# The gate projection placed inside the decode attention of a hybrid decoder step

## The reference

```python
h = rmsnorm(x, norm_pre_mix)
q_f, k_f, v_f, f_logit, q_d, k_d, v_d = split(h @ w_in)          # 8 fox heads, 3 x 4 dilated heads, 128 wide
o_fox = softmax(q_f k_f^T / sqrt(128) + forget bias) @ v_f        # sample: 2048 cached tokens in 16 pages of 128, per request
o_dil = windows (128,1), (512,4), (2048,16), merged by their denominators
g_fox, g_dil = split(sigmoid(h @ w_gate + b_gate))                # 2048 x 4096
m = (g_fox * (o_fox @ w_o_fox) + g_dil * (o_dil @ w_o_dil)) @ w_out
x = x + rmsnorm(m);  y = x + rmsnorm(swiglu(rmsnorm(x)))          # 2048 x 11264, 5632 x 2048
```

## Time and profile before

| what | value |
|---|---|
| median of 3 runs | 2866.8 us (2862.89 to 2868.53) |
| the profiled execution, its own time | 2874.63 us |
| its span, first to last instruction | 2872.7 us |
| mean granted clock | 0.919 |
| PE busy | 88 % of the span |
| DVE, ACT, POOL busy | 36 %, 30 %, 14 % |
| moved by DMA | 574.66 MB |

### The profile page before, as it was taken

The page is one execution under the profiler, slowest core; times in us unless marked ns, Lnnn a source line. Parts: engine busy times, 40 slices in busy tenths (PEclk is TensorE's granted clock), DMA queues, the critical chain, the costliest instruction groups (busy, mean ns, idle before and its releaser), DMA issues.

```text
span 2872.7 us, 46489 instructions
## 1 busy us (share of the span) xinstructions
PE 2515.9 (88%) x18285; PEld 2246.4 (78%) x18285; DVE 1048.4 (36%) x1391; ACT 857.5 (30%) x970; POOL 408.2 (14%) x846
## 2 busy tenths in 40 slices
PE   5799579995599968888888789689999999899996
PEld 4799369994499954454554789489999999899995
DVE  1343224432233433333332453533333333344444
ACT  2123112331034422322222222334343343333322
POOL 1000000001100024443343000001111111022210
PEclk8699569997599989999999899899999999999998
DMA  6144104552044359999999454347767666578881
GB/s 169 58 153 154 53 30 146 161 155 94 21 124 146 117 180 361 366 379 340 349 349 384 134 175 155 107 154 240 240 233 243 235 234 228 196 240 278 288 274 58
DMA packets 332581, 574.66 MB, mean 200 GB/s; under 512 B 19251, under 2 KB 277579, under 8 KB 328479
## 3 DMA queue, kind: packets, MB, share of 16 engines
q1 hardware_dynamic: 263520, 269.62, 29.8%
q0 software_dynamic: 68960, 303.67, 29.5%
HBM read 558.77 MB, written 104.10 MB: 231 GB/s over the span
## 4 chain that ended last, share of the span: by engine, by line
PE 75%; DMA 9%; issue 5%; DVE 5%; ACT 2%; POOL 2%; POOLq 2%; SPq 0%; DVEq 0%; ACTq 0%
PE ps L638 20%; PE ps L639 20%; PE ps L640 20%; DMA kraw<-in_cache_fox_k 4%; PE ps L647 2%; PE ps L809 2%; DMA kraw<-in_cache_win_k 1%; DMA vraw<-in_cache_fox_v 1%; POOLq L534 1%; PE ps L814 1%; PE ps L899 1%; PE ps L834 1%; ACT w_hi L1005 1%; DMA d_h<-scratch_hankel 1%; DMA raw<-in_w_down 1%
## 5 line engine op out<-in xcount | busy, mean ns | idle before, releaser
L638 PE MATMUL ps<-act_hi,w_hi 128*128 128x320 f32 x3136 | 976.8, 311 | 31.1 <-DVE act_lo L1307 22.5
L1278 DVE TENSOR_TENSOR w_lo<-raw,w_hi 128x2048 fp32r<-128x2048 f32 (+2 forms) x276 | 582.7, 2112 | 1088.4 <-ACT w_hi L1005 1088.4
L639 PE MATMUL ps<-act_lo,w_hi 128*128 128x320 f32 x3136 | 973.2, 310 | 0.0
L640 PE MATMUL ps<-act_hi,w_lo 128*128 128x320 f32 x3136 | 972.8, 310 | 0.0
L1005 ACT ACTIVATE w_hi<-raw 128x2048 fp32r<-128x2048 f32 (+2 forms) x276 | 487.9, 1769 | 993.5 <-PE ps L640 975.3
L638 PEld LDWEIGHTS ps<-act_hi,w_hi 128*128 128x128 f32 x3136 | 592.7, 189 | 32.1 <-issue 32.1
L639 PEld LDWEIGHTS ps<-act_lo,w_hi 128*128 128x128 f32 x3136 | 592.6, 189 | 0.0
L640 PEld LDWEIGHTS ps<-act_hi,w_lo 128*128 128x128 f32 x3136 | 592.4, 189 | 0.0
L1508 DVE COPY kT<-ps 128x512 f32<-128x512 f32 x176 | 121.8, 692 | 280.2 <-PE ps L814 280.2
L1150 ACT ACTIVATE kT<-ps 128x512 f32<-128x512 f32 x184 | 109.8, 597 | 323.6 <-PE ps L809 323.5
L809 PEld LDWEIGHTS ps<-ident,kraw 128*128 128x128 f32 x736 | 80.3, 145 | 154.8 <-DMA kraw<-in_cache_fox_k 78.8
(11 more groups left out here) (305 smaller groups left out, 2597.6 us busy)
## 6 DMA issues: line engine op xcount, KB each, us to landing
raw<-in_w_gate_up SPq DMA_DIRECT2D x88, 1024.0 KB, 7.4
kraw<-in_cache_fox_k POOLq DMA_DIRECT2D x128, 512.0 KB, 7.7
vraw<-in_cache_fox_v POOLq DMA_DIRECT2D x128, 512.0 KB, 7.9
raw<-in_w_in SPq DMA_DIRECT2D x60, 1024.0 KB, 7.6
raw<-in_w_gate SPq DMA_DIRECT2D x32, 1024.0 KB, 6.6
raw<-in_w_down SPq DMA_DIRECT2D x32, 1024.0 KB, 5.9
out_win_k_sample<-in_cache_win_k POOLq DMA_DIRECT2D x64, 510.0 KB, 5.8
out_win_v_sample<-in_cache_win_v POOLq DMA_DIRECT2D x64, 510.0 KB, 3.9
```

The source lines that it names most:

```text
L638: pe.matmul(ps[:, bk_, 0:T], w_hi[:, slot, k, :], xh[:, x_k, :], start=(k == k0), stop=False)
L639: pe.matmul(ps[:, bk_, 0:T], w_hi[:, slot, k, :], xl[:, x_k, :], start=False, stop=False)
L640: mm = pe.matmul(ps[:, bk_, 0:T], w_lo[:, slot, k, :], xh[:, x_k, :], start=False, stop=(k == k1 - 1))
L1278: dve.tensor_tensor(w_lo[:, slot, 0:kt, :], raw[:, pslot, 0:kt, P * half:P * half + P], w_hi[:, slot, 0:kt, :].bitcast(F32), ALU.subtract) ...
```

## The change

The gate units leave their stage and are placed whole after steps of decode: two in sequence 0 and in sequence 8, four in each other one, so at steps 5, 11, 17, 23 (11, 23 for two). A unit's result goes through a two-slot tile gst to DRAM; the sigmoid reads PSUM with the bias in the same instruction. A unit's weight split is in two halves, after the next step and after the one behind it. Panels all use raw's slot 0. act_hi, act_lo, raw slot 0, w_hi and w_lo stay whole, so decode's tiles move elsewhere: the key ring has 3 slots, the value ring 4 (in raw's slot 1). The attention output is kept as one fp32 tile, o32; its prompt part is split to o_hi and o_lo in sequence 8, the rest at the end. The o units' gates are loaded from DRAM by POOL into four slots. In the diff `gate_part` is PE's, last in each step of `sequence`; `gate_out` and `gate_split` are ACT's, and DVE has the same `gates_after` with its subtraction in place of the cast. `prompt_lo` is called at steps 5 to 7 of sequence 8, after ACT's `prompt_hi`.

```diff
-        o_hi = sb("o_hi", [P, HF + HG, T], F32R, M0 + 20480)
-        o_lo = sb("o_lo", [P, HF + HG, T], F32R, M0 + 35840)
+        o32 = sb("o32", [P, HF + HG, T], F32, M0 + 20480)
+        o_hi = sb("o_hi", [P, HF + HG, T], F32R, X0)
+        o_lo = sb("o_lo", [P, HF + HG, T], F32R, X0 + 16384)
...
-        KRING, VRING = 4, 8
+        KRING, VRING = 3, 4
+        vraw = sb("vraw", [P, VRING, 1024], F32, B0 + 57344)
+        gst = sb("gst", [P, 2, T], F32, Y0 + 9216)
+        gl = sb("gl", [P, 4, 2, T], F32, M0 + 35840)
-        gates = sb("gates", [P, 2 * KT, T], F32, X0)
...
+        GATE_UNITS = (2, 4, 4, 4, 4, 4, 4, 4, 2)
+        def gate_work(q, n):
+            u0, units = U_GATE + sum(GATE_UNITS[:q]), GATE_UNITS[q]
+            ended = range(units * n // STEPS, units * (n + 1) // STEPS)
+            return [(u0 + m, k) for m in ended for k in range(KT)]
+        def gates_done(q, n, late):
+            return [U_GATE + m for m, step_ in enumerate(GATE_DONE) if step_ + 1 + late == STEPS * q + n]
...
-            stream(U_GATE, 2 * KT, lambda i, s: (w_gate, i * 512 + 256 * s))
-            sp.wait_ge(o_ev, DB)
+            for p in range(KT):
+                for u in range(U_GATE + 2 * p - 4, U_GATE + 2 * p - 2):
+                    if u >= U_GATE:
+                        sp.wait_ge(acc_free, u + 3)
+                        sp.dma_start(gsc[u - U_GATE], gst[:, u % 2, :]).then_inc(g_st[u % 2], 16)
+                load_panel(0, U_GATE + 2 * p, [(0, cols_of(w_gate, 256 * p, 0, 8)), (8, cols_of(w_gate, 256 * p, 8, KT))])
...
+            sp.wait_ge(pv_done, DB * KPG)
+            load_panel(1, U_O, [(0, wof[:, :, 256:512]), (8, wod[:, :, 256:512])])
...
-            pool.wait_ge(acc_free, U_O + 2)
-            pool.wait_ge(zero_ok, 1)
+            pool.wait_ge(lo_done, U_GATE)
...
             def load_bias(b):
+                pool.wait_ge(zero_ok, 1)
...
+            pool.wait_ge(g_st[0], 16 * KT)
+            pool.wait_ge(g_st[1], 16 * KT)
...
+            with pool.Fori(0, KT // 4) as i:
+                for k in range(4):
+                    pool.wait_ge(acc_free, i * 4 + (U_O + k - 1))
+                    pool.dma_start(gl[:, k], halves[bass.ds(i * 4 + k, 1)].rearrange("e p o t -> p (e o) t")).then_inc(g_ld[k], 16)
...
+            def gate_part(q, n):
+                for u, k in gate_work(q, n):
+                    if k == 0:
+                        pe.wait_ge(lo_done, u + 1)
+                        pe.wait_ge(acc_free, u + 1)
+                    acc = ps[:, u % 2, 0:T]
+                    pe.matmul(acc, w_hi[:, u % 2, k, :], act_hi[:, k, :], start=(k == 0), stop=False)
+                    pe.matmul(acc, w_hi[:, u % 2, k, :], act_lo[:, k, :], start=False, stop=False)
+                    mm = pe.matmul(acc, w_lo[:, u % 2, k, :], act_hi[:, k, :], start=False, stop=(k == KT - 1))
...
-            pe.wait_ge(o_ev, DB)
+            pe.wait_ge(acc_free, U_O + 2)
+            pe.wait_ge(o_sp, 1)
...
+            def gate_out(u):
+                act.wait_ge(unit_done, u + 1)
+                wait_pos(act, g_st[u % 2], 16 * ((u - U_GATE) // 2))
+                act.activation(gst[:, u % 2, :], ps[:, u % 2, 0:T], ACT.Sigmoid,
+                               bias=cols[:, 64 + u - U_GATE:65 + u - U_GATE]).then_inc(acc_free, 1)
+            def gate_split(u, late):
+                if not late:
+                    act.wait_ge(raw_ld[0], loads(U_GATE) + 32 * ((u - U_GATE) // 2 + 1))
+                ks = slice(8, KT if u < U_O else KO) if late else slice(0, 8)
+                act.activation(w_hi[:, u % 2, ks, :], raw[:, 0, ks, P * (u % 2):P * (u % 2) + P], ACT.Copy).then_inc(hi_done if late else g_half, 1)
+            def gates_after(q, n):
+                for u in gates_done(q, n, 0):
+                    gate_out(u)
+                    gate_split(u + 2, False)
+                for u in gates_done(q, n, 1):
+                    gate_split(u + 2, True)
...
-            def out_parts(h, src, done):
-                link(dve.tensor_copy(hi, src))
-                dve.tensor_tensor(lo, src, hi.bitcast(F32), ALU.subtract).then_inc(done, 1)
+            def keep_out(h, src, done):
+                dve.tensor_copy(o32[:, bass.ds(h, 1), 0:SEQ].rearrange("p o n -> p (o n)"), src).then_inc(done, 1)
...
+            def prompt_lo(c):
+                dve.wait_ge(os_h, c + 1)
+                part = (slice(None), slice(4 * c, 4 * c + 4), slice(0, SEQ))
+                dve.tensor_tensor(o_lo[part], o32[part], o_hi[part].bitcast(F32), ALU.subtract)
...
+                    dve.wait_ge(g_ld[k], i * 16 + 16)
+                    dve.tensor_tensor(a1, ps[:, k, 0:T], gl[:, k, 0, :], ALU.mult)
```

More of the change, by code:

```diff
@@ L795, in _ @@
             pe.wait_ge(pre_ok, 1)
[L798 to L801 removed]
+            def gate_part(q, n):
[7 more added lines that the diff above has]
+                    mm = pe.matmul(acc, w_lo[:, u % 2, k, :], act_hi[:, k, :], start=False, stop=(k == KT - 1))
+                    if k == KT - 1:
+                        mm.then_inc(unit_done, 1)
             def transposes(b, s):
@@ L929, in turn_out, with sequence @@
                 mm.then_inc(o_tr, 1)
-            def sequence(kb, vb):
-                for n in range(KPG + 1):
+            def sequence(q, kb, vb):
+                for n in range(STEPS):
                     if kb is not None and n < KPG:
@@ L1127, in _ @@
                     act.activation(d_pt[:], ps[:, 3 + g, 0:384], ACT.Copy).then_inc(pd_pc, 1)
-            def gate_trip(i, last):
-                for k in range(4):
-                    if last and k >= 2:
-                        act.wait_ge(unit_done, i * 4 + (U_GATE + k + 1))
-                    else:
-                        step(i * 4 + (U_GATE + k), k, i * 32 + loads(U_GATE))
-                    act.wait_ge(acc_free, i * 4 + (U_GATE + k + 3))
-                    g = gates[:, bass.ds(i * 4 + k, 1), :].rearrange("p o n -> p (o n)")
-                    act.activation(g, g, ACT.Sigmoid).then_inc(g_sig, 1)
-            with act.Fori(0, 2 * KT // 4 - 1) as i:
-                gate_trip(i, False)
-            gate_trip(2 * KT // 4 - 1, True)
+            def gate_out(u):
[14 more added lines that the diff above has]
+                    gate_split(u + 2, True)
+            act.wait_ge(fb_st, 16 * DB)
             def keys_a(b, s):
@@ L1463, in _, with gate_split, gates_after @@
             dve.wait_ge(fb_st, 16 * DB)
-            def gate_trip(i, last):
-                for k in range(4):
-                    if last and k >= 2:
-                        dve.wait_ge(unit_done, i * 4 + (U_GATE + k + 1))
-                    else:
-                        step(i * 4 + (U_GATE + k), k)
-                    dve.tensor_scalar(gates[:, bass.ds(i * 4 + k, 1), :].rearrange("p o n -> p (o n)"), ps[:, k, 0:T],
-                                      cols[:, bass.ds(i * 4 + (k + 64), 1)], None, ALU.add).then_inc(acc_free, 1)
-            with dve.Fori(0, 2 * KT // 4 - 1) as i:
-                gate_trip(i, False)
-            gate_trip(2 * KT // 4 - 1, True)
+            def gate_split(u, late):
+                dve.wait_ge(hi_done, u + 1) if late else dve.wait_ge(g_half, u - U_GATE - 1)
+                ks = slice(8, KT if u < U_O else KO) if late else slice(0, 8)
+                ins = dve.tensor_tensor(w_lo[:, u % 2, ks, :], raw[:, 0, ks, P * (u % 2):P * (u % 2) + P],
+                                        w_hi[:, u % 2, ks, :].bitcast(F32), ALU.subtract)
+                if late:
+                    ins.then_inc(lo_done, 1)
+            def gates_after(q, n):
+                for u in gates_done(q, n, 0):
+                    gate_split(u + 2, False)
+                for u in gates_done(q, n, 1):
+                    gate_split(u + 2, True)
             dve.memset(pg[:], 0.0)
```

127 lines of the change are left out of this document (71 added, 56 removed).

## The result

The changed kernel takes 2893.9 us (median of 6 runs, 2883.1 to 2901.2), the kernel before 2867.3 in the same comparison: ratio 1.0087, 95% interval 1.007 to 1.0103. It is slower by 0.9 %, and the prediction (2820, range 2778 to 2872) has the wrong sign and misses the time by 74 us. The profiled execution took 2893.58 us.

A forecast was written before the change was run, and what follows sets the result against it. After the change TensorE (84 us a sequence) was to bound decode, with DMA (79) close behind. Savings 226.0 - 15 - 167 - 15 + 8.6 + 2.8 + 6.5 = 46.9 us, less 7.8 for the median, gave 2820 us, range 2778 to 2872.

The forecast's parts named there:

- Part 3: Decode sequences 1 to 7: walked six steps at a time to 88.6 us, plus 2.4, so 91 against 67.1; 167 us given back.
- Rival D: Decode: units not overlapping with transfers at all; ruled out because no ring slot waits for a unit; no chance given.
- The floors: Decode, per sequence: least time from each engine's own work, TensorE 84.1 us with four units, DMA about 79 us.
- Rival B: Decode: gate panel lands too late, ScalarE waits ahead of key evictions; 70 us more, 2890; chance 0.13.
- Rival C: Decode: shallow rings, each unit costs 3 us of a fresh landing; 96 us a sequence, 35 more, 2855; chance 0.12.
- Rival A: Decode: TensorE alone bounds, panel stalls vanish; 86 us a sequence, 35 us less, 2785; chance 0.22.
- Part 1: Before decode: the gate stage goes, first transpose near 800.3 instead of 1026.33, 226.0 us earlier.
- part 6: Prompt heads: out_parts becomes one copy, 12 x 0.54 = 6.5 us saved; the prompt's later split costs nothing, 6 at most.
- Part 2: Decode sequence 0, keys alone: two units add 14 us, smaller ring 5, refilling during a unit takes off 4; 15 more.
- Part 4: Decode sequence 8, values alone: two units 14.0 us, value ring of four 3, refill takes off 2; 15 more.
- Part 5: Turn from decode to o projection: 14.6 us becomes about 6, 8.6 saved, and 2.8 saved from low-clock matmuls.
- Table loads: Decode ScalarE: four loads of 1.28 us a sequence, about half exposed; with a drain 39 us more, 2859, chance 0.04.

The follow-up runs named there:

- e11: Changed kernel with gate units spread evenly over steps, splits after even units three steps later, and an eighth of each gate panel from the third on: 2788.0 us.
- e12: Changed kernel with units spread evenly, splits after even units three steps later, and key and value rings of 4 and 8 (act_hi used twice): 2772.8 us.
- e10: Changed kernel with an eighth of each gate panel from the third on and key and value rings of 4 and 8 (act_hi used twice): 2815.5 us.
- e1: Changed kernel loading only an eighth of each gate panel from the third on, all waits kept: 2866.5 us.
- e2: Changed kernel with one matmul of 48 in each gate unit, panels, splits and rings kept: 2828.5 us.
- e3: Changed kernel with key and value rings of 4 and 8 instead of 3 and 4 (act_hi used twice): 2927.4 us.
- e9: Changed kernel with an eighth of each gate panel from the third on and one matmul of 48 in each unit: 2711.8 us.
- e8: Kernel before with key and value rings of 3 and 4 instead of 4 and 8, nothing else: 2927.2 us.
- e7: Changed kernel with units' blocks spread evenly over the steps and splits after even units three steps later, whole panels, rings 3 and 4: 2805.0 us.
- e4: Changed kernel with Exp in place of Sigmoid on the gates, which leaves no table loads in decode: 2884.3 us.
- e6: Changed kernel with the weight split after each even unit three steps later, units still whole: 2878.0 us.
- e13: Kernel before with the value ring alone cut from eight slots to four, key ring kept at four: 2887.7 us.

## Why the prediction was wrong

**Part 3 is the step that failed**, with 53.9 of the 65.7 us by which the first projection matmul is late (1620.5 for 1554.8). It forecast that the seven sequences would give back 167 us of the gain, at 91 us each; they take 98.7. By the experiments, from the floor up: 85.2 floor (e11, e12), + 4.4 for whole units with rings of four and eight (e10), + 5.3 for rings of three and four (e1), + 3.8 for the panel (after). The first step holds two edits, the whole units and their early splits; the others hold one each. The order matters, as e2, e3 and e9 show, so these are prices along one path and not shares. In TensorE's own account the 13.5 us above the floor are 9.8 of idle time (98.7 - 88.9) and 3.7 of busy time more than the floor, for which I had nothing. The low clock can account for them: a mean granted clock of 0.95 over the sequences, between levels of 0.5 and 1 (1.2 and 2.4 GHz), is nearly 10 us of each at the lower level.

Within part 3: I had written that rings of three and four hold one unit's worth of DMA work, and charged 2.4 us for everything beyond the walk. The walk took each engine's sum over six steps, which is right only if the loads keep coming while TensorE is in a unit. They don't, since a slot is freed by TensorE and POOL issues in order (5.96 us without an issue at 994.72). Rival D said the opposite in so many words, that no ring slot waits for a unit; this was the mistake behind the walk. The ring's price in the kernel before is 7.2 us (e8) where I had 0. In sequence 0 I had priced the same cut at 1.8 us a step against 1.3; in the steady sequences I didn't ask.

**The floors held.** TensorE 85.2 against 84.1. For the DMA engines I had 79; 0.96 x 87.9 in e7 are 84, within a few us of TensorE's. So both were near their limit. That the two can run there together is shown by e12; what the prediction had no term for is what it takes.

**Rival B** had the right verdict and the right picture: the wait of ScalarE on raw<-in_w_gate, the eviction behind it, the panel started after the late split. Its turn-taking estimate of 26 us is for the 128 packets of a whole panel on each engine, and a whole panel takes 21.7 us here and 24.6 in e12, where the DMA engines are full. ScalarE comes for it after 20.7 us where I had 17 to 20, so it waits in 5 panels, at most 4.1 us, and not up to 9 in each. Its price was too high, 3.8 us a sequence here where I had 70 / 7 = 10; that its total of 2890 comes near the result is luck, and the rings' doing. In the flight of a panel some 1700 key and value packets of 4 KB pass beside some 2200 on the panel's queue in e12, and some 1280 beside 2100 in the changed kernel. The Trainium skill, DMA: Bandwidth & Descriptors, section Queues, rings and completion order, has each engine take turns between the queue rows packet by packet. The trace agrees that both share the engines; in its own packets the turns are not one for one, but not far from it in e12. **Rival C** was nearest in the number, 96 us a sequence, for a reason that is half right: the rings, but by the slots that a unit keeps occupied and not by a landing of 3 us after each. **Rival A**, 86 us, is what e11 and e12 reach, and e7 within 2 us, once both stalls are gone.

**Part 1 and part 6** held: 233.7 us against 232.5. **Part 2**: 5.2 us short; rings cost there what I said (e8 takes 58.6 where the kernel before takes 54.5), and by that sum the unit gave nothing back for refilling, the 4 us that I took off. This is one execution; e4 and e6 do the same sequence in 3.5 us less. **Part 4**: 7.6 short; the value ring costs 10.9 us at the end (e13) and not 3. **Part 5**: the turn held to 0.2 us, in part by luck. The last unit's sigmoid and the split behind it stand ahead of the last copies of o in the queues of ScalarE and VectorE and take 3.3 us of it (0.53, 0.95 and 1.83), for which I had nothing, and what I had listed takes less than I thought. The low clock did not go. **Part 7**: nothing seen. **Table loads**: e4 gives 1.4 us a sequence, within the 2.4.

Beside the kernel before, in the two profiled executions: 233.7 us earlier at the first transpose, then 20.5 later in sequence 0 (76.2 for 55.7), 220.9 in the seven (690.9 for 470), 22.6 in sequence 8 (54.6 for 32), and 8.8 and 2.2 earlier at the turn and after it. That is 19.3 us slower, and the spans are 2892.0 and 2872.7. Taken by the marks alone the seven sequences are 216 us longer (98.7 for 67.8); the other 4.7 come from the boundaries 1082 and 1552, which are not at the marks of the kernel before.

What stays open: the 4.4 us of whole units with deep rings (e10) are 3.5 of idle time, most of it behind late key evictions by the two rows above, and 0.9 of busy time at a mean clock of 0.98. How much of the idle time would go with a full clock I can't say; no run holds the clock. Nor is there a run with whole units and late splits at deep rings, which would part the two edits of the first step.

## What to carry to other kernels

Before laying one stage's engine work over another stage's transfers, read by whom the slots of the issuing queue are freed: a burst on that engine stops the loads, which sums of busy time don't show. How long the queue stands for a slot (141 us here) says that the ring is full and that a smaller one may be felt; it is no measure of the loss, since e12 has 325.7 us of it at the floor. Spread the added work evenly, and let the reader of a big load come late; compare the time at which it comes with the time at which the load lands. Do both at once: spreading alone moved the stall to the panel, the later reader alone left the stall on the keys (28 and 16 us alone, 89 together). And when a change shrinks a buffer to pay for its memory, run the old kernel with the small buffer alone: it is one line, and here it showed a term of 62 us.

## What was not expected of the hardware

In the kernel before, one slot of 4 KB a partition in the key ring, from four to three, costs 6.5 us of 67.8, while four slots of the value ring cost 1.2. Half a panel, 1 MB, lands (median of both halves) in 6.6 us beside an idle software queue and in 18 to 19 us beside a busy one, with each packet at its old price of 50 ns. TensorE's granted clock fell to the lower level in an idle time of 4.97 us at the turn to the projection and behind one of 3.14 us at 1000.14 inside a sequence. It fell 13 times in the seven sequences of the changed kernel, seven of them behind idle times of at most 1.72 us, and not once in those of e12.
